# The high and low parts of gated outputs in places of their own, split during the gate products

## The reference

```python
oa = oa * jax.nn.silu(z_sb)                                   # first layer
ob = ob * jax.nn.silu(z_r)
x = x + gate * (jnp.concatenate([oa, ob], -1) @ w_out)        # 2048 rows
...
y_a = y_a * jax.nn.silu(sc_z)                                 # even layer
y_b = rms(y_b * jax.nn.silu(ssd_z))
y_m = memory_attention(mq, mem_n, w_mk, w_mv) * jax.nn.silu(mz)
x = x + jnp.concatenate([y_a, y_b, y_m], -1) @ w_out0         # 3584 rows
...
y_c = causal_block_attention(q_full, k_full, v) * jax.nn.silu(z_c)
y_m = memory_attention(mq, mem_n, w_mk, w_mv) * jax.nn.silu(mz)
x = x + jnp.concatenate([y_c, y_m], -1) @ w_out1              # 2560 rows
```

## Time and profile before

| | |
|---|---|
| median of 3 runs | 1843.25 us (1837.95 to 1847.15) |
| the profiled execution | 1844.38 us, of which 1842.6 us span |
| TensorE busy | 1768.5 us, 96% of the span |
| VectorE busy | 1260.2 us, 68% |
| ScalarE busy | 899.7 us, 49% |
| GpSimd busy | 112.4 us, 6% |
| mean granted TensorE clock | 0.984 of full speed |

### The profile page before, as it was taken

The page is one execution under the profiler, slowest core; times in us unless marked ns, Lnnn a source line. Parts: engine busy times, 40 slices in busy tenths (PEclk is TensorE's granted clock), DMA queues, the critical chain, the costliest instruction groups (busy, mean ns, idle before and its releaser), DMA issues.

```text
span 1842.6 us, 24254 instructions
## 1 busy us (share of the span) xinstructions
PE 1768.5 (96%) x9667; PEld 1505.0 (82%) x9667; DVE 1260.2 (68%) x1604; ACT 899.7 (49%) x1158; POOL 112.4 (6%) x146
## 2 busy tenths in 40 slices
PE   5899999999999989999999999999899999999897
PEld 4688888877887878888888888788788888887786
DVE  6879978785677565886667667854474567576654
ACT  4444443444555445675444666634354445455542
POOL 2311101000100000110000000000000000000000
PEclk9999999999999999999999999999999999999999
DMA  9989969774445546666555556565556565444453
GB/s 323 348 307 337 338 221 329 228 238 131 144 149 166 188 136 187 193 185 181 161 144 146 163 155 181 161 193 184 179 151 170 171 184 148 121 122 124 135 186 103
DMA packets 311840, 350.56 MB, mean 190 GB/s; under 512 B 11232, under 2 KB 286816, under 8 KB 311728
## 3 DMA queue, kind: packets, MB, share of 16 engines
q1 hardware_dynamic: 297792, 298.34, 53.5%
q0 software_dynamic: 13936, 50.67, 7.7%
HBM read 346.87 MB, written 2.10 MB: 189 GB/s over the span
## 4 chain that ended last, share of the span: by engine, by line
PE 87%; DVE 6%; ACT 2%; issue 2%; DMA 2%; POOL 0%; SPq 0%; DVEq 0%; ACTq 0%
PE psG L468 47%; PE psG L469 24%; PE psG L462 2%; PE psG L463 2%; PE psG L464 2%; DVE w_lo L402 1%; ACT w_hi L398 1%; PE psH L1704 1%; DMA raw<-in_mem_w 1%; PE psH L1693 1%; PE psH L1718 1%; DMA ada_ring<-in_w_ada 1%; PE psH L1996 1%; PE psH L1997 1%; DVE gate_sum L1133 1%
## 5 line engine op out<-in xcount | busy, mean ns | idle before, releaser
L468 PE MATMUL psG<-xA,w_hi 128*128 128x512 f32 x3392 | 1223.1, 404 | 25.8 <-issue 19.7
L469 PE MATMUL psG<-xA,w_lo 128*128 128x256 f32 x3392 | 954.2, 281 | 0.0
L402 DVE TENSOR_TENSOR w_lo<-raw,w_hi 128x1024 fp32r<-128x1024 f32 (+1 forms) x560 | 687.0, 1239 | 291.4 <-ACT w_hi L398 289.9
L468 PEld LDWEIGHTS psG<-xA,w_hi 128*128 128x128 f32 x3392 | 642.1, 189 | 187.7 <-issue 33.1
L398 ACT ACTIVATE w_hi<-raw 128x1024 fp32r<-128x1024 f32 (+1 forms) x560 | 570.7, 1044 | 284.7 <-PE psG L469 225.7
L469 PEld LDWEIGHTS psG<-xA,w_lo 128*128 128x128 f32 x3392 | 645.6, 190 | 3.9 <-issue 3.4
L437 ACT ACTIVATE P<-psG 128x512 f32<-128x512 f32 x102 | 60.6, 594 | 251.0 <-PE psG L469 251.0
L1095 DVE TENSOR_TENSOR P<-psG,P 128x512 f32<-128x512 f32 (+2 forms) x103 | 70.4, 684 | 121.8 <-ACT P L437 119.6
L560 POOL TENSOR_TENSOR W<-W 128x512 f32<-128x512 f32 x15 | 22.2, 1480 | 1016.2 <-ACT W L613 1016.2
L1133 DVE SCALAR_TENSOR_TENSOR ada_sum<-ada_ring,silc,ada_sum 128x1024 f32<-128x1024 f32 x60 | 77.8, 1302 | 0.0
L571 POOL DMA_DIRECT2D ada_ring<-in_w_ada x96 | 50.9, 531 | 326.5 <-DVE ada_sum L1133 134.1
(11 more groups left out here) (304 smaller groups left out, 1738.6 us busy)
## 6 DMA issues: line engine op xcount, KB each, us to landing
raw<-in_w_in SPq DMA_DIRECT2D x360, 512.0 KB, 3.8
raw<-in_w_out SPq DMA_DIRECT2D x128, 512.0 KB, 3.4
ada_ring<-in_w_ada POOLq DMA_DIRECT2D x96, 512.0 KB, 6.1
raw<-in_mem_w SPq DMA_DIRECT2D x32, 512.0 KB, 8.9
raw<-in_w_uq SPq DMA_DIRECT2D x24, 384.0 KB, 3.3
raw<-in_w_ukv SPq DMA_DIRECT2D x32, 128.0 KB, 2.5
raw<-in_w_ukv SPq DMA_DIRECT2D x16, 256.0 KB, 3.4
P<-in_memT SPq DMA_DIRECT2D x4, 512.0 KB, 5.6
```

The costliest lines, as they stand in the source:

```text
L402: nc.vector.tensor_tensor(low(n), low(n, raw), high(n), ALU.subtract).then_inc(lo_ready, 1)
L468: nc.tensor.matmul(psG[:, bank + f, :], hi[:, w], x, start=first, stop=False)
L469: last = nc.tensor.matmul(psG[:, bank + f, S:2 * S], lo[:, w], x[:, 0:S], start=False, stop=end)
```

## The change

The parts of gated outputs get places of their own. `yP` is a view of all 81 tiles of `P` as `F32R`; two neighbouring tiles take one tile's high and low part. `Y1`, `Y2` and `Y3` list such pairs, in tiles that are dead by then: in the first layer those of `SBV`, `SBZ`, `SBQ`, `RTV`, in the second of `SSZ`, `XS`, `SSB`, `SSC`, `SCC`, `SCV`, in the odd one the keys and values of the heads of the same group. The memory attention's output of the odd layer goes to `yM`, over tiles 8 to 15 of `memkv`. Since `xA` isn't written, the waits for the last gate product go, and the splits of all groups but the last move into the gate stages. Where a group's places are those of an earlier group's output, ScalarE waits for that group's low part. In the first layer the multiplication by z is made ahead of the sigmoid (`times_z_1`). In the odd layer the gate of the memory attention's output is made in the first pass of `G_ZC` instead of in `G_OUT1`.

```diff
+Y1 = [16 + 2 * k for k in range(8)] + [2 * k for k in range(4)] + [48 + 2 * k for k in range(4)]
+Y2 = [32 + 2 * k for k in range(12)] + [64 + 2 * k for k in range(4)] + [56 + 2 * k for k in range(4)] + [8 + 2 * k for k in range(8)]
+Y3 = [24 + 2 * k for k in range(16)]
...
-        xB = sb("xB", [NP, 12, 2 * S], F32R, place=in_p(0))
+        yP = sb("yP", [NP, NTILE, S], F32R, place=in_p(0))
+        yM = sb("yM", [NP, 4, 2 * S], F32R, place=kv_place + 8 * S * 4)
...
+        def from_p(places):
+
+            return lambda k: yP[:, places[k]:places[k] + 2, :].rearrange("p t s -> p (t s)")
+
+        def y_parts(places, k, n):
+
+            t = places[k]
+            return yP[:, t:t + 2 * n:2, :], yP[:, t + 1:t + 2 * n:2, :]
...
-        G_OUT = Gemm(KT, 8, columns(io["w_out"], 0), from_a, ready=lambda tiles: (q["f1_lo"], tiles // 4), pair=True)
+        G_OUT = Gemm(KT, 8, columns(io["w_out"], 0), from_p(Y1), ready=lambda tiles: (q["f1_lo"], tiles // 4), pair=True)
...
-                      ready=lambda tiles: (q["f3_lo"], tiles // 4), pair=True)
+                      ready=lambda tiles: (q["f3_lo"], tiles // 4) if tiles <= KT else (q["m3_lo"], 1), pair=True)
...
             def hi_1(g):
                 act.wait_ge(q["f1_y"], g + 1)
-                f(hA[:, 4 * g:4 * g + 4, :], P[:, GATED1[g][0]:GATED1[g][0] + 4, :], ACT.Copy).then_inc(q["f1_hi"], 1)
+                if g == 2:
+                    act.wait_ge(q["f1_lo"], 2)
+                f(y_parts(Y1, 4 * g, 4)[0], P[:, GATED1[g][0]:GATED1[g][0] + 4, :], ACT.Copy).then_inc(q["f1_hi"], 1)
...
-                if n == 3 and p == 15:
-                    products_done(act, G_RTZ)
-                    hi_1(0)
+                if p == 1 and n >= 2:
+                    hi_1(n - 2)
...
-                if p == 2:
+                if p == 0:
                     landed(act, G_RTZ)
                     log_1(3)
-                if p == 6:
+                if p == 4:
                     sigmoid(gate_buf(3), "f1", 4)
-                if p in (1, 3, 9):
-                    hi_1((1, 3, 9).index(p) + 1)
+                if p in (2, 8):
+                    hi_1((2, 8).index(p) + 2)
...
+                if g in (2, 4):
+                    act.wait_ge(q["f2_lo"], g)
...
-                if v == 1 and p == 15:
-                    products_done(act, G_CB)
-                    hi_2(0)
+                if (v, p) in ((0, 11), (0, 14), (1, 5), (1, 11)):
+                    hi_2(((0, 11), (0, 14), (1, 5), (1, 11)).index((v, p)))
...
-                if p in (1, 4, 6, 13, 15, 18):
-                    hi_2((1, 4, 6, 13, 15, 18).index(p) + 1)
+                if p in (10, 12, 15):
+                    hi_2((10, 12, 15).index(p) + 4)
...
             def zc_hook(b, p):
                 mla_hook(4 * b + p // 4, p % 4)
-                if p == 3 and b >= 1:
+                if b == 0:
+                    if p == 3:
+                        log_part(gate_3_buf, tiles(MZ, 4)).then_inc(q["gate_log"], 1)
+                    if p == 7:
+                        sigmoid(gate_3_buf, "m3", 1)
+                    if p == 12:
+                        act.wait_ge(q["m3_y"], 1)
+                        f(yMH, P[:, MQ:MQ + 4, :], ACT.Copy).then_inc(q["m3_hi"], 1)
+                    return
+                if p == 3:
                     z_log(b - 1)
-                if p == 7 and b >= 1:
+                if p == 7:
                     sigmoid(gate_3_buf, "zc", b)
-                if b == 3 and p == 15:
-                    products_done(act, G_ZC[1])
-                    hi_3(0)
+                if p == 11:
+                    hi_3(b - 1)
...
+            def times_z_1(g):
+
+                y, z = tiles(GATED1[g][0], 4), tiles(GATED1[g][1], 4)
+                landed(dve, *((G_SBZ, 2 * g + 2) if g < 2 else (G_RTZ, 2 * g - 2)))
+                dve.wait_ge(*((q["sb_y"], 4) if g < 2 else (q["rt_y"], 2 * g - 2)))
+                v.tensor_tensor(y, y, z, ALU.mult).then_inc(q["f1_yz"], 1)
...
             def z1_hook(n, p):
                 rt_hook(n, p)
+                if p == 2 and n:
+                    times_z_1(n - 1)
                 if p == 5 and n:
                     sigmoid_1(n - 1)
                 if p == 13 and n:
                     gate_1(n - 1)
+                if p == 4 and n >= 2:
+                    lo_1(n - 2)
...
+                if (n, p) in ((0, 13), (0, 15), (1, 7), (1, 13)):
+                    lo_2(((0, 13), (0, 15), (1, 7), (1, 13)).index((n, p)))
...
+                if p == 13:
+                    lo_3(b - 1)
...
-                if p == 8:
-                    dve.wait_ge(q["gate_log"], GATE["zc"] + 5)
-                    log_sigmoid(gate_3_buf, tiles(MZ, 4)).then_inc(q["gate_lsig"], 1)
-                if p == 11:
-                    dve.wait_ge(q["gate_sig"], GATE["zc"] + 5)
-                    link(v.tensor_tensor(gate_3_buf, tiles(MZ, 4), gate_3_buf, ALU.mult))
-                    v.tensor_tensor(tiles(MQ, 4), tiles(MQ, 4), gate_3_buf, ALU.mult).then_inc(q["f3_y"], 1)
-                if p in (1, 5, 10, 14):
-                    lo_3((1, 5, 10, 14).index(p) + 1)
+                if p == 9:
+                    lo_3(3)
```

More of the change, by code:

```diff
@@ L929, in out0_hook @@
             def out0_hook(b, p):
-                if b == 1 and p == 6:
-                    act.wait_ge(q["f2_y"], 1)
                 squares_3(b, p)
@@ L1032, in out1_hook @@
                     z_log(3)
-                if p == 6:
-                    act.wait_ge(q["zc_done"], 4)
-                    log_part(gate_3_buf, tiles(MZ, 4)).then_inc(q["gate_log"], 1)
-                if p in (5, 10):
-                    sigmoid(gate_3_buf, "zc", 4 if p == 5 else 5)
-                if p in (1, 4, 9, 13):
-                    hi_3((1, 4, 9, 13).index(p) + 1)
+                if p == 5:
+                    sigmoid(gate_3_buf, "zc", 4)
+                if p == 8:
+                    hi_3(3)
             run(G_OUT1, out1_hook)
@@ L1506, in out0_hook @@
                     v.tensor_tensor(tiles(MQ, 4), tiles(MQ, 4), W[:, 0:1024], ALU.mult)
-                if p == 10:
+                if p == 8:
                     landed(dve, G_CB)
@@ L1631, in zc_hook, with lo_3 @@
                 mla_hook(4 * b + p // 4, p % 4)
-                if p == 5 and b >= 1:
+                if b == 0:
+                    if p == 5:
+                        dve.wait_ge(q["gate_log"], GATE["m3"] + 1)
+                        log_sigmoid(gate_3_buf, tiles(MZ, 4)).then_inc(q["gate_lsig"], 1)
+                    if p == 9:
+                        dve.wait_ge(q["gate_sig"], GATE["m3"] + 1)
+                        link(v.tensor_tensor(gate_3_buf, tiles(MZ, 4), gate_3_buf, ALU.mult))
+                        v.tensor_tensor(tiles(MQ, 4), tiles(MQ, 4), gate_3_buf, ALU.mult).then_inc(q["m3_y"], 1)
+                    if p == 13:
+                        dve.wait_ge(q["m3_hi"], 1)
+                        v.tensor_tensor(yML, P[:, MQ:MQ + 4, :], yMH, ALU.subtract).then_inc(q["m3_lo"], 1)
+                    return
+                if p == 5:
                     z_log(b - 1)
-                if p == 9 and b >= 1:
+                if p == 9:
                     z_factor(b - 1)
                     gate_3(b - 1)
+                if p == 13:
+                    lo_3(b - 1)
+            def lo_3(g):
+                dve.wait_ge(q["f3_hi"], 2 * g + 2)
+                for u in range(2):
+                    t = QT + 3 * (2 * g + u)
+                    hi, lo = y_parts(Y3, 4 * g + 2 * u, 2)
+                    ins = v.tensor_tensor(lo, P[:, t:t + 2, :], hi, ALU.subtract)
+                ins.then_inc(q["f3_lo"], 1)
             for u in range(2):
                 run(G_ZC[u], lambda b, p: zc_hook(2 * u + b, p))
-            def lo_3(g):
-                dve.wait_ge(q["f3_hi"], 2 * g + 2)
-                dve.wait_ge(q["f3_y"], g + 1)
-                for u in range(2):
-                    t = MQ + 2 * u if g == 4 else QT + 3 * (2 * g + u)
-                    if g == 4:
-                        hi, lo = kvH[:, 2 * u:2 * u + 2, :], kvL[:, 2 * u:2 * u + 2, :]
-                    else:
-                        k = 4 * g + 2 * u
-                        hi, lo = hA[:, k:k + 2, :], lA[:, k:k + 2, :]
-                    ins = v.tensor_tensor(lo, P[:, t:t + 2, :], hi, ALU.subtract)
-                ins.then_inc(q["f3_lo"], 1)
             def out1_hook(b, p):
```

68 lines of the change are left out of this document (30 added, 38 removed).

## The result

The changed kernel takes 1829.79 us (median of 17 runs, 1823.14 to 1838.44), the kernel before beside it 1847.33 us (17 runs, 1837.95 to 1854.36). The ratio is 0.9907, with a 95% interval of 0.9890 to 0.9925: 0.93% faster, by about 17 us. The profiled execution has a span of 1826.7 us, 15.9 us under that of before, where the prediction had the sum 16.0.

The account below looks back on a forecast made before the run. TensorE, busy for 96% of the span, was taken as the bound. 22.3 us of stops and slow clock less new stops of 1.2, 3.9 and 1.2 us gave 16.0 us, so 1827 us, range 1818 to 1836.

Parts of the forecast that it names:

- the sum: Whole kernel: 22.3 us of stops and slow clock less new stops of 1.2, 3.9 and 1.2 us, 16.0 us gained.
- The stops and the clock that go (22.3 us): Output products: five TensorE stops, 14.9 us, and 7.4 us lost to slow clock, the most the change can take away.
- The first layer: Gate stage and `G_OUT`: new stops of 0.5 us twice and 0.2 us, 1.2 us, against 3.53 + 1.55 gone.
- The second layer: Gate stage and `G_OUT0`: stops of 1.4, 1.4, 0.4 and 1.2 us; 3.9 us new against 3.54 + 1.55 gone.
- The odd layer: Gate stage 0 us; in `G_OUT1` one new 1.2 us stop at the seventh chunk, waiting for the last group's chain.
- the largest free item of the sum: Odd gate stage: three groups' parts, 2.4 us each, and the memory block's 9.8 us fit into idle time, 0 us.
- the terms 9.4, 1.3, 1.15, 1.14 and 1.3 us: `G_OUT1`, last group: logarithm to last gating, the gating itself, high part, weight split and low part, said to end at 1719.7.
- Nothing new waits: Rival, all three layers: the moved chains end in time and bring no new stop; 1821 us, chance 0.12.
- the new stops cost more than their length: Rival: vector queue later than counted, or close stops bring the clock down; two slow stretches, 2 us lateness, 1832 us, chance 0.18.
- The first chunks wait all the same: Rival, output products: first chunks wait for the bank, stops shrink only to some 2.5 us; 1837 us, chance 0.07.
- The slower one: Rival, gate stages: VectorE's and ScalarE's queue bounds, 29.6 us of inserted work shows in full; 1850.5 us, chance 0.03.
- the 7.4 us that I gave to the clock: Output products: four slow stretches, 16.38 us at clock 0.50, each losing 0.45 of its length, should go.

Follow-up runs that it names:

- the second layer alone: The kernel before with only the second layer's part of the change; 1839.0 us in the profiled execution.
- the kernels above: The changed kernel with the second layer's second low part moved behind `SCC*SCV`, 1824.3 us, or made twice at its place, 1825.3 us (profiled executions).
- the kernel with this layer's splits in idle time: The changed kernel with the second layer's high and low parts moved to where ScalarE and VectorE idle or into `G_OUT0`; 1824.6 us in the profiled execution.
- The kernel with the wait dropped: Kernel before with parts in own places, no waits for the last gate product, first parts at the gate stage's last position, other splits unmoved; 1838.8 us profiled.
- the later comparison: The changed kernel once more (its second profile), beside the kernel before on one chip; 1831.28 us (8 runs) against 1846.24 us, ratio 0.9927.
- the twelve kernels of the table: The kernel before, the changed kernel, its repeat and nine experimental variants, one profiled execution each; 1823.9 to 1844.4 us.
- the kernel with the places alone: The kernel before with the parts in their own places, every wait for a gate product and every position unchanged; 1842.6 us in the profiled execution.
- one low part twice: The changed kernel with the second layer's low part of the second group made twice at its place; 1825.3 us in the profiled execution.
- the odd layer alone: The kernel before with only the odd layer's part of the change; 1833.8 us in the profiled execution.

## Why the prediction was right

*The stops and the clock that go (22.3 us).* All five stops went and no slow stretch is left in the three stretches. What a slow stretch costs was right as well: with the stop of 3.53 us kept and no slow clock behind it (the second layer alone) the first layer's stretch is 1.6 us shorter than in the kernel before, for 1.55 in the sum.

*The first layer.* I had 0.5 us twice and 0.2 us. The recorded stops are 0.25 us in the third retention step and 0.05 us in `G_OUT`, but TensorE's matmuls lie 0.53 us later behind the third step than in the kernel before, and 0.95 us later when the fourth is done too. The gain was 3.8 us for 3.9. With the low parts behind `rt_at` that lateness is gone and the stretch is 1.0 us shorter still, so that was the right chain.

*The second layer.* Predicted stops of 1.4, 1.4, 0.4 and 1.2 us, measured 1.37, 1.09, none and 0.90. The lateness of the product is shown by the kernels above, 1.14 us for each low part ahead of it, one for one. The recorded stops make 2.9 us new for the 3.9 of the sum. Held against the kernel with this layer's splits in idle time, which has only the old stop, the changed kernel is 4.0 us late at the 6201st matmul, of which some 0.5 is another pace. So the new lateness is about 3.5 us, and the term was right within half a us. The layer gained 1.45 us up to there for the 1.2 of the sum; the 0.25 us over its whole stretch is this less the slower pace behind.

*The odd layer.* 1.2 us predicted, 0.96 measured, in every kernel with this layer's part as it stands, and no stop over 0.1 us in its gate products. That the memory chain and three groups of splits fit in there for nothing was the largest free item of the sum, and it held. But the working of the 1.2 us has a slip that another one hides. From 1704.4, the terms 9.4, 1.3, 1.15, 1.14 and 1.3 us make 1718.7, not 1719.7, and that would be 0.2 to 0.6 us behind what TensorE wants. In the changed kernel (ScalarE's logarithm, VectorE's gating, VectorE's low part):

```profile
1700.42 1.05 ACT L667 ACTIVATE memkv<-P 128x1024 f32<-128x1024 f32 x1
```

```profile
1709.79 0.69 DVE L1651 TENSOR_TENSOR P<-P 128x512 f32<-128x512 f32 x1
...
1714.39 0.68 DVE L1681 TENSOR_TENSOR yP<-P,yP 128x512 fp32r<-128x512 f32 x1
```

The logarithm to the gating takes 9.4 us, as counted. Between the end of the high part (1712.26) and the low part lie 2.1 us for the one weight split of 1.14, so the chain is 15.3 us long and not 14.3. The forecast of this stop came out by luck.

*Rivals.* "Nothing new waits" and "the new stops cost more than their length" are both out: the stops are there, none of them has a slow stretch behind it. "The first chunks wait all the same" is wrong for this change. The kernel with the wait dropped has stops of about that size (1.30, 2.61 and 2.10 us), but they end with the first low part and not with the bank: VectorE's addition for the bank runs from 1165.28 to 1165.96, and TensorE starts `G_OUT0` at 1165.46. The slower one, with all inserted work on the path, is far off. The change inserts about 30 us of work into the gate stages, and some 5 us of it show.

*What made the sum better than its terms.* That the profiled execution met the forecast within 0.1 us is luck. The pace of the matmuls took 1.2 us in the last 600 of the second layer's stretch and gave 0.5 us in the last 400 of the odd one's (69.6 us for 70.1); the odd layer had gained 11.6 us by the 9201st matmul for the 11.0 of the sum. The medians say the same with less luck in them: the changed kernel is 17.5 us faster over 17 runs and 15.0 us in the later comparison, for 16.0.

## What to carry to other kernels

When a wait is removed, ask what stands in front of the freed work in its in-order queue; here the wait was 2.2 us of the first stop, but only 0.9 of each of the next two. Work moved under TensorE's cover was free where its queue had idle rows. Ahead of an operation on whose result another engine's queue waits, it made that operation late by its full issue distance, one for one; so put it right behind that operation. Read what TensorE lost from the starts of its matmuls, since a recorded idle time is shorter. And compare stages over equal numbers of matmuls, since totals of single executions differ by more than a change of this size.

## What the runs showed of the hardware

**The pace of a stream of matmuls has two values at the full clock.** The windows of the kernel before and of the changed one over the same product, `G_OUT0`, at clock 1.00:

```profile
1220.00:1260.00 40.00, 40.00 (x233) 35.28 (x232) 21.01 (x19) 15.81 (x15) 2.13 (x2) 1.00 0.61 193
```

```profile
1220.00:1260.00 40.00, 40.00 (x229) 34.73 (x227) 20.23 (x19) 15.80 (x15) 2.13 (x2) 1.00 0.59 186
```

233 matmuls in 40 us against 229, 2% apart. The 40 matmuls from the 6241st on take 6.93 us in six of the twelve kernels of the table and 7.06 to 7.08 us in the other six. It isn't the place of the inputs. The changed kernel's second profile has 232 in the same window, and in the kernel with the places alone the slow pace stands in a product of the second layer that no kernel here touches, where 400 matmuls took 70.67 us against 69.34 in the changed kernel:

```profile
726.32:796.99 70.67, 70.67 (x402) 61.25 (x401) 56.34 (x73) 46.19 (x57) 7.21 (x3) 1.00 0.65 186
```

```profile
725.70:795.04 69.34, 69.34 (x403) 61.14 (x402) 56.02 (x72) 46.46 (x56) 7.24 (x3) 1.00 0.66 190
```

Those 400 matmuls take 69.3 us in seven of the kernels and 70.7 us in five. Here a stream kept its pace for hundreds of matmuls and changed it at an interruption, sometimes without any in sight. What chooses it stays open; none of the kernels here was made for that question.

**The clock does not follow every stop.** Behind 3.53 us before `G_OUT` the clock fell in the kernel before, but in the kernel with the second layer alone the same stop had full clock behind it, and the first layer's stretch was 1.6 us shorter for it:

```profile
559.47 0.47 PE L482 MATMUL psG<-xA,w_hi 128*128 128x512 f32 x1 [3.53 <-issue]
```

```profile
559.50:566.00 6.50, 6.50 (x37) 5.70 (x38) 4.62 (x5) 5.82 (x6) 0.00 (x0) 1.00 0.24 81
```

In the same execution the stop of 3.04 us before `G_OUT1` (at 1699.57) had none either. In the kernels that keep them, ten of the twelve stops of 3.0 to 3.5 us before the output products had a slow stretch behind them, and all five of 4.2 to 4.3 us. The stop of 2.61 us (before `G_OUT0`, wait dropped) had one (clock 0.66 over the next 5 us); those of 2.31 us (one low part twice), 2.10 and 1.30 us (wait dropped) had none. Outside the changed stages one of 2.28 us did (the odd layer alone, at 317.93, clock 0.50 from 320.46 to 323.87). So the 7.4 us that I gave to the clock are what that one execution paid, and another can pay less. The same holds outside the changed stages: the 400 matmuls from the 801st on, the same in all kernels, took 76.67 us at clock 0.96 in the kernel before, and 73.46 us at full clock in the kernel with the odd layer alone.
